# Latent attention on one core: scores of two-part operands in three passes, and the first probabilities turned ahead of the query

## The reference, cut to what matters

```
MLA_HEADS, MLA_NOPE, MLA_ROPE, MLA_V = 16, 64, 32, 64   # 96 query and key dims
q = rms_norm_2(q, q_gain)                 # (1, 512, 16, 96)
k = rms_norm_2(k, k_gain)
q = concatenate([q[..., :64], apply_rope(q[..., 64:], pos)])
k = concatenate([k[..., :64], apply_rope(k[..., 64:], pos)])
sc = einsum('bqhd,bkhd->bhqk', qi, k) * 96 ** -0.5    # blocks of 128 queries
mask = key_chunk[None, :] <= q_chunk[:, None]          # chunks of 64
p = softmax(where(mask, sc, -inf))
o = einsum('bhqk,bkhd->bqhd', p, v)
```

## Time and profile before

| | |
|---|---|
| median of 3 runs | 2076.73 us (2076.71 to 2079.87) |
| profiled execution, its own time | 2079.63 us |
| its span, first to last instruction | 2077.7 us |
| PE busy | 2048.6 us, 99% |
| DVE busy | 943.5 us, 45% |
| ACT busy | 843.7 us, 41% |
| mean granted PE clock | 0.999 of 2.4 GHz |

### The profile page before, as it was taken

The page is one execution under the profiler, slowest core; times in us unless marked ns, Lnnn a source line. Parts: engine busy times, 40 slices in busy tenths (PEclk is TensorE's granted clock), DMA queues, the critical chain, the costliest instruction groups (busy, mean ns, idle before and its releaser), DMA issues.

```text
span 2077.7 us, 26912 instructions
## 1 busy us (share of the span) xinstructions
PE 2048.6 (99%) x11129; PEld 1759.7 (85%) x11129; DVE 943.5 (45%) x1327; ACT 843.7 (41%) x1173; POOL 21.9 (1%) x38
## 2 busy tenths in 40 slices
PE   7999999999999999999999999999999999999999
PEld 7889888889888888897889888888878899888887
DVE  5744453325543343566664343443543345434343
ACT  4332233333433332557764333333555534333332
POOL 1000000000000000010000000000000000000000
PEclk9999999999999999999999999999999999999999
DMA  7222222232332333220112332333222212233232
GB/s 230 72 72 81 72 64 69 84 109 92 102 101 82 101 101 101 74 57 32 41 42 63 101 99 86 99 101 101 82 81 62 81 62 87 96 101 99 86 99 84
DMA packets 169688, 178.98 MB, mean 86 GB/s; under 512 B 6769, under 2 KB 139454, under 8 KB 169346
## 3 DMA queue, kind: packets, MB, share of 16 engines
q1 hardware_dynamic: 168424, 176.58, 26.9%
q0 software_dynamic: 1024, 1.12, 0.2%
q10 hardware_dynamic: 154, 0.04, 0.0%
HBM read 174.50 MB, written 2.10 MB: 85 GB/s over the span
## 4 chain that ended last, share of the span: by engine, by line
PE 93%; DVE 3%; ACT 2%; issue 1%; DMA 0%; SPq 0%; DVEq 0%; ACTq 0%
PE psum L82 28%; PE psum L84 28%; PE psum L83 28%; PE psum L1828 1%; PE psum L1806 1%; PE psum L762 1%; PE psum L740 1%; PE psum L2238 1%; DVE weights_lo L318 1%; PE psum L431 1%; PE psum L748 1%; ACT weights_hi L312 0%; PE psum L1816 0%; PE psum L2217 0%; DVE small L1970 0%
## 5 line engine op out<-in xcount | busy, mean ns | idle before, releaser
L82 PE MATMUL psum<-norm_T_hi,weights_hi 128*128 128x512 f32 (+1 forms) x1440 | 538.7, 374 | 1.5 <-DVE scratch L989 0.8
L84 PE MATMUL psum<-norm_T_hi,weights_lo 128*128 128x512 f32 (+1 forms) x1440 | 533.5, 371 | 0.0
L83 PE MATMUL psum<-norm_T_lo,weights_hi 128*128 128x512 f32 (+1 forms) x1440 | 533.2, 370 | 0.0
L82 PE MATMUL psum<-weights_hi,act_T_hi 128*128 128x512 f32 (+2 forms) x976 | 366.5, 376 | 5.5 <-issue 1.6
L84 PE MATMUL psum<-weights_hi,act_T_lo 128*128 128x512 f32 (+2 forms) x976 | 364.4, 373 | 0.0
L83 PE MATMUL psum<-weights_lo,act_T_hi 128*128 128x512 f32 (+2 forms) x976 | 364.3, 373 | 0.0
L1351 ACT ACTIVATE weights_hi<-raw_weights 128x2048 fp32r<-128x2048 f32 x92 | 175.7, 1909 | 342.3 <-PE psum L84 342.3
L82 PEld LDWEIGHTS psum<-norm_T_hi,weights_hi 128*128 128x128 f32 x1440 | 271.3, 188 | 50.2 <-issue 2.8
L84 PEld LDWEIGHTS psum<-norm_T_hi,weights_lo 128*128 128x128 f32 x1440 | 271.2, 188 | 46.6
L83 PEld LDWEIGHTS psum<-norm_T_lo,weights_hi 128*128 128x128 f32 x1440 | 271.4, 188 | 45.3
L1447 DVE TENSOR_TENSOR weights_lo<-raw_weights,weights_hi 128x2048 fp32r<-128x2048 f32 x92 | 210.9, 2292 | 106.7 <-ACT weights_hi L1351 106.7
(11 more groups left out here) (253 smaller groups left out, 1925.5 us busy)
## 6 DMA issues: line engine op xcount, KB each, us to landing
raw_weights<-in_ffn_w_dram SPq DMA_DIRECT2D x64, 1024.0 KB, 5.3
raw_weights<-in_w_in_dram SPq DMA_DIRECT2D x36, 512.0 KB, 4.7
raw_weights<-in_w_up_dram SPq DMA_DIRECT2D x16, 1024.0 KB, 5.6
raw_weights<-in_w_down_dram SPq DMA_DIRECT2D x16, 1024.0 KB, 4.9
raw_weights<-in_w_in_dram SPq DMA_DIRECT2D x12, 1024.0 KB, 5.1
raw_weights<-in_mlstm_w_in_dram SPq DMA_DIRECT2D x8, 1024.0 KB, 5.0
raw_weights<-in_w_out_dram SPq DMA_DIRECT2D x4, 1024.0 KB, 5.1
raw_weights<-in_mla_w_o_dram SPq DMA_DIRECT2D x4, 1024.0 KB, 5.1
```

What stands on the lines that cost most here:

```text
L82: pe.matmul(out, ah, bh, start=start, stop=False)
L83: pe.matmul(out, ah, bl, start=False, stop=False)
L84: return pe.matmul(out, al, bh, start=False, stop=stop)
```

## The change

The operands of the scores are kept as high and low parts, and each score tile is made with `mm3` from F32R parts instead of one full-precision matmul. The high parts are what ACT writes (in place of QT and KT, now of type F32R); the low parts are made by a new DVE step `turned_lo(j, h)`, 32 in all: four ahead of the first mask, and in the pass for head n two for head n+2. `turned_lo` reads the PSUM bank of its job, so a job two places later waits for it as well, and `scores` waits for it instead of for ACT. The parts lie in parts of act_T_hi, act_T_lo and key_rows that nothing else uses at that time. Second, PE runs `turn(n, 0)` before the transposes of query n+2 and no longer after them.

```diff
-        KEYROWS = sb("key_rows", [P, 1024])
+        KEYROWS = sb("key_rows", [P, 1024], F32R)
...
+            KROWS = KEYROWS[0:MQK, :].rearrange("p (b s) -> p b s", b=2)
+            QKH = [[AH[0:MQK, 5, :], AH[0:MQK, 6, :]], [KROWS[:, 0, :], KROWS[:, 1, :]]]
+            QKL = [[AL[0:MQK, 5, :], AL[0:MQK, 6, :]], [AH[0:MQK, 7, :], AL[0:MQK, 7, :]]]
...
                         if order[m - 2][0] == "out":
                             pe.wait_ge(tl.sem, tl.at(order[m - 2][1] + 1))
+                        if order[m - 2][0] == "tr":
+                            pe.wait_ge(trl.sem, trl.at(2 * order[m - 2][2] + order[m - 2][1] + 1))
...
                 def scores(n):
-                    pe.wait_ge(ev.sem, ev.at(emptied[idx[("tr", 1, n)]]))
+                    pe.wait_ge(trl.sem, trl.at(2 * n + 2))
...
-                        pe.matmul(PS[:, b, c:c + w], QT[:, n % 2, t * P:t * P + P], KT[:, n % 2, 0:w],
-                                  start=True, stop=True).then_inc(sc.sem, 1)
+                        tt = slice(t * P, t * P + P)
+                        mm3(pe, PS[:, b, c:c + w], QKH[0][n % 2][:, tt], QKL[0][n % 2][:, tt],
+                            QKH[1][n % 2][:, 0:w], QKL[1][n % 2][:, 0:w], True, True).then_inc(sc.sem, 1)
...
                     scores(n + 1)
+                    turn(n, 0)
                     for what in behind:
                         job(what)
-                    turn(n, 0)
                     turn(n, 1)
...
-                        act.activation((QT, KT)[j][:, h % 2, :], src[0:MQK, :], ACT.Copy, scale=GC[:, j:j + 1]).then_inc(ev.sem, 1)
+                        act.activation(QKH[j][h % 2], src[0:MQK, :], ACT.Copy, scale=GC[:, j:j + 1]).then_inc(ev.sem, 1)
...
+                def turned_lo(j, h):
+                    m = idx[("tr", j, h)]
+                    dve.wait_ge(ev.sem, ev.at(emptied[m]))
+                    dve.scalar_tensor_tensor(QKL[j][h % 2], PS[0:MQK, bank(m), :], GC[:, j:j + 1],
+                                             QKH[j][h % 2].bitcast(F32), MUL, SUB).then_inc(trl.sem, 1)
...
                 norm(0)
+                for h in range(2):
+                    for j in range(2):
+                        turned_lo(j, h)
                 mask(0, 3)
...
                     dve.tensor_copy(PT[:, 4 * P:8 * P], PS[:, 4, :]).then_inc(a1.sem, 1)
+                    if n + 2 < MH:
+                        turned_lo(0, n + 2)
                     if n + 1 < MH:
                         masks(n + 1)
+                    if n + 2 < MH:
+                        turned_lo(1, n + 2)
                     if n % 2 == 0 and n:
                         out_lo(n // 2 - 1)
```

More of the change, by code:

```diff
@@ L287, in build @@
         drained = count("heads_gated")
+        trl = count("query_key_lo")
         cleared = count("constants_set")
@@ L1702, in mla @@
             SB = SCR[:, 12448:13728]
-            QT = SCR[0:MQK, 13728:14752].rearrange("p (b s) -> p b s", b=2)
             RT = SCR[:, 14752:15776].rearrange("p (c t h f) -> p c t h f", c=2, t=NT, h=4)
-            KT = KEYROWS[0:MQK, :].rearrange("p (b s) -> p b s", b=2)
+            KROWS = KEYROWS[0:MQK, :].rearrange("p (b s) -> p b s", b=2)
+            QKH = [[AH[0:MQK, 5, :], AH[0:MQK, 6, :]], [KROWS[:, 0, :], KROWS[:, 1, :]]]
+            QKL = [[AL[0:MQK, 5, :], AL[0:MQK, 6, :]], [AH[0:MQK, 7, :], AL[0:MQK, 7, :]]]
             ssum, mean, root, rstd = (SM[:, i * 32:i * 32 + 32] for i in range(4))
@@ L1759, in _ @@
             @block.tensor
-            def _(pe, ev=ev.copy(), tl=tl.copy(), pex=pex.copy(), a1=a1.copy(), pte=pte.copy(), ond=ond.copy(), fs=fs.copy(), ropes=ropes.copy()):
+            def _(pe, ev=ev.copy(), tl=tl.copy(), pex=pex.copy(), a1=a1.copy(), pte=pte.copy(), ond=ond.copy(), fs=fs.copy(), ropes=ropes.copy(), trl=trl.copy()):
                 def job(what):
@@ L2097, in mla @@
             xn.passed(4); sq.passed(8); ms.passed(12); rt.passed(4); rs.passed(4); v1.passed(8); fs.passed(4); fr.passed(16)
-            qsc.passed(4); cleared.passed(1)
+            qsc.passed(4); cleared.passed(1); trl.passed(2 * MH)
             def freed(pe, j, t):
```

## The result

The changed kernel takes 2089.82 us in the median of four runs (2088.40 to 2091.26); the kernel before, now four runs too, 2077.56 (2076.71 to 2079.87). The ratio is 1.0057, 95% interval 1.0045 to 1.0068: **slower by 11.8 us** by the ratio (the medians are 12.3 apart), where +6.6 us and 2083.3 us were forecast. The direction was right; the time lies above the range.

A forecast was written before the change was run, and what follows sets the result against it. PE or DVE bounds the kernel depending on the head, so terms went head by head: 4.0 + 3 x 0.37 + 2 x 0.16 - 2 x 0.32 + 0.69 + 1.45 - 0.35 = +6.6 us, median 2083.3, range 2078.5 to 2087.

The forecast's parts named there:

- The sum keeps one such dip: Behind PE's wait at 966 us: one half-clock stretch of 3.4 us, costing 1.5 us, stays as before.
- more dips: Rival: added waits, several in heads 9 to 12, bring half clock once or twice more, +1.5 each; 2085 to 2087; chance 0.15.
- the +1.45 that the sum had for heads 8 to 10: 0.69 in head 9, then head 10's exponentials wait for a delayed shift and PE for head 11's low parts.
- PE's scores at 1.90 us: Every head: three passes take 1.90 us in place of 2.21, a gain of 0.31 us a head.
- The step's duration and pace: DVE's `turned_lo`, 32 times: pace 0.67 us, span 0.75.
- The start, +1.35: Ahead of the first mask: low parts wait for ACT's copies and hold PE's transposes, so the mask starts 1.35 us later.
- two steps in each of passes 0 and 1, +2.7: Heads 0 and 1: DVE has no gap, so four low-part steps of 0.67 us count in full, 2.7 us.
- Odd late heads bound by the key's low part, even ones by the query's: Scores wait for the key: +0.16 in heads 11, 13; "out" waits for the query: +0.37 in heads 2, 6, 12.
- Head 3's -0.32: Head 3, as head 7: four projections stand between and cover the wait for the key's low part, a gain of 0.32 us.
- Heads 4 and 5, +0.69: DVE is late for head 6's mask; reordering starts head 5's mask 0.7 earlier, two low parts add 1.34: +0.69 us.
- cover: Rival: DVE steps find room in every head, only the scores count; decided at the start; -5.0 us, 2071.7; chance 0.05.
- a wash: Rival: start costs 4.0, later waits are covered and 11 heads gain 0.31; +0.6, 2077.3, with half about 2080; chance 0.25.

The follow-up runs named there:

- e5: Changed kernel plus 28 idle transposes of the identity set into three PE waits; 2085.44 us, ratio 1.0032 to the kernel before.
- e1: Kernel before with only the reordering, the first turn ahead of the query's transposes; 2076.23 us, ratio 0.9988.
- e10: Kernel before with the reordering and nine idle transposes ahead of pass 1's projections; 2076.00 us, ratio 0.9987.
- e2: Changed kernel without the reordering, the first turn put back behind the query's transposes; 2094.07 us, ratio 1.0075 to the kernel before.
- e3: Changed kernel without low parts and their waits, the three passes reading high parts only; 2073.84 us, ratio 0.9976 to the kernel before.
- e8: Low parts and three-pass scores in seven heads only, full precision in the other nine, reordering in all; 2076.92 us, ratio 0.9993 to the kernel before.
- e11: Kernel before with reordering, nine idle transposes, and three-pass scores in heads 5, 9, 13, 15, low parts made in odd passes; 2075.56 us, ratio 0.9982.
- e9: Kernel before with nine idle transposes ahead of pass 1's projections; 2077.37 us, ratio 0.9994.
- e4: Changed kernel with full-precision scores; low-part steps, their waits and the reordering stay, results unused; 2090.28 us, ratio 1.0058 to the kernel before.
- e7: Changed kernel with each low-part step over 64 of 512 columns, all waits and places kept; 2078.09 us, ratio 0.9996 to the kernel before.
- e6: Changed kernel with the same 32 low-part steps at other places in VectorE's list; 2087.58 us, ratio 1.0044 to the kernel before.

## Why the prediction was wrong

The step that failed is the one on the clock: "The sum keeps one such dip". The changed kernel has two stretches at half clock, each about 7 us and not 3.4, and they lie where PE sets the pace or comes to set it by being slow. With PE's waits filled (e5) there is no half clock, and the kernel is faster by 4.4 us in the median and by 4.1 in the table, 1.4 of it in 0-1 and 1-2 and 2.8 in 9-10. So the clock costs over 4 us where the sum kept 1.5. This was the rival "more dips", given 0.15 and priced at +1.5 each "as in rows 9", which gave 2085 to 2087 and was too low as well. The error is in that price as much as in the chance: a stretch's length was taken as fixed, and it ran for 3.4, about 7 and about 10 us in different kernels. In 9-10 the forecast had waits of 0.85 us worked out ahead of the scores and did not ask what PE's clock would do behind them. That pass at full clock is 9.71, +1.55 on before, near the +1.45 that the sum had for heads 8 to 10.

The rest of the sum was too low as well. e5 is 6.6 us slower than before, the very number of the forecast, but that is luck: e5 has no half clock, and the sum keeps the dip of before on both sides. With that dip out of before (12.72 in e1 less 11.15 in e10, 1.57 us) e5 is 7.9 us longer by the table, and its median is 8.2 over before's executions with a mean clock of 1.000. So the terms other than the clock came to about 8 us for 6.6; 0.8 of the difference lies behind values(10) and 0.3 ahead of values(2). By the table the 10.4 us are 6.6 forecast, 1.2 by these terms and 2.6 by the clock beyond the dip that was kept. The ratio's 11.8 us has an interval from 9.3 to 14.1, so what lies between it and 10.4 is not to be explained from one trace each.

Point by point:

- PE's scores at 1.90 us: right where they follow `values` at once, 1.96 from 1062.88 to 1064.84. Behind a wait they take 2.18 (1069.52 to 1071.70), and hardly anything of the gain on 2.21 is left. 96 rows run at the pace of 128 (0.23 for 512 columns, 0.17 for 384).
- The step's duration and pace: right (0.74 and 0.67).
- The start, +1.35: right, the first mask begins 5.20 us behind the first transposes of a query for 3.86. With two steps in each of passes 0 and 1, +2.7: right in sum. The table has +1.26 for values(0) and +2.91 for 0-1 and 1-2, together 4.17 against 4.05. Part of it is luck. The dip of before, 1.5 us behind the weight split, has moved ahead of it; with no dip (e5) the three together are 2.76 over before, which has one, so 4.33 with the clock full in both.
- Odd late heads bound by the key's low part, even ones by the query's: right in kind, the next scores 6.64 us and "out" 5.02 us (1074.54) behind the start of the scores, for 6.62 and 4.72. The size for passes 11 to 14 was 0.34 and is 1.01 (in the table from values(10) to values(15)): a term is missing from the sum, the 0.27 us that the first pass of the scores takes longer behind a wait, which came in passes 12 and 14, and pass 14 gained nothing.
- Head 3's -0.32: wrong, 2-3 is 9.58 for 9.60. ScalarE's weight split stands ahead of the first copy there and ends at 987.8, so the turn, over by 987.0, was copied only then; head 7 has no split and gained 0.33.
- Heads 4 and 5, +0.69: +0.63 by the chain (1011.16 against 1007.87, and 1.51 for the earlier start, less the 4.17 so far).
- The reordering was not priced alone. It is worth 2.5 us to the kernel before (e1) and 4.3 to the changed one (e2, with a third stretch at half clock in it).
- Rival "cover": its place was right (e3, without low parts, gives 5.0 us), its condition not: the low parts are covered nowhere but in a few odd passes (e8, e11).
- Rival "a wash": its time with half of the gain was worked out wrong, 4.0 less 1.7 on 2076.7 is 2079.0 and not about 2080; nothing hangs on it.

What stays open is what decides where the half clock begins. Each stretch that was looked at begins near a PE wait of 0.9 to 1.9 us, between 0.8 us before the wait's end (1051.5 for 1052.26, kernel after) and 2.3 us behind it (956.6 for 954.33 in e9). But waits of the same length are also passed without it: 1.12 us up to 955.46 and 1.61 up to 970.50 in the changed kernel, and 0.99 in e4 ahead of the scores at 1054.85. The Trainium skill, "TensorE: Matmul & The Clock Gate", Part 1, says of the rise to full clock in sustained work that its moment varies from run to run. That the clock of one and the same kernel differs between executions is seen here too, in before's 26 of 61 with a mean of 1.000; no run here shows where in the other 35 it fell.

## What to carry to other kernels

When an edit takes work from one engine and gives it to another, cost the new work pass by pass: the same 0.67 us was free in an odd pass (e11), cost its whole length in passes where VectorE leads, and held up TensorE through a bank that it kept in even ones. When a change adds waits of about a microsecond to TensorE, put the half clock behind them into the sum and into the range, with more than one length; here a profile with one such stretch was followed by one with two, each twice as long. And when an experiment lands on the forecast's number, check that both count the same things before calling the rest of the sum right. Last, take the two parts of a change apart: the order of one line gave 2.5 us here, and the arithmetic with its low parts took 14.

## What the runs showed of the hardware

- Idle transposes can make a kernel faster: 28 of them, about 3 us of PE work set into waits, took 4.4 us off the changed kernel (e5), with clock 1.00 in place of 0.50 over 14 us.
- A stretch at half clock lasted 3.4 us (before, e1, e4, e7, e8), about 7 (after, e6, e9) and about 10 (e3), each near a PE wait of 0.9 to 1.9 us; waits of 1.12 and 1.61 us in the changed kernel had none.
- Executions of one kernel differ in it: 26 of 61 of before have a mean clock of 1.000 (median 2077.2 us), the others 0.998 or 0.999 (2079.6).
- After a wait the first 512-column pass holds the chain for 0.50 us, where the next ones take 0.23 (kernel after, 1069.52).
- VectorE's step with a gain column from PSUM takes 0.27 us for 64 columns and 0.74 for 512, so, if the time grows evenly with the width, an estimated 0.2 of it does not depend on it.
